# Attention of the latent (MLA) layer: the scaling of the probabilities moved ahead of the row maximum on VectorE, and the next heads' projections spread one to a step

## The reference

```python
def mla_mixer(xn, w_dq, q_norm, w_uq, w_o, k_nope, k_rope, v, cos, sin):
    c_q = rmsnorm(xn @ w_dq, q_norm)
    q = (c_q @ w_uq).reshape(bsz, seq, MLA_HEADS, MLA_NOPE + MLA_ROPE)      # 16 heads, 128 + 64
    q_nope = q[..., :MLA_NOPE]
    q_rope = apply_rope(q[..., MLA_NOPE:], cos[:, None, :], sin[:, None, :])
    # per block of 128 queries
    s = einsum('bqhd,bkhd->bhqk', qn, k_nope) + einsum('bqhr,bkr->bhqk', qr, k_rope)
    s = where(key_pos <= q_pos, s * scale, -inf)
    p = softmax(s, axis=-1)
    o = einsum('bhqk,bkhv->bqhv', p, v)
    return o @ w_o
```

## Time and profile of the kernel before

| | |
|---|---|
| median of 3 runs | 2618.04 us (2617.62 to 2619.24) |
| the profiled execution | 2625.55 us, of which its span 2623.4 us |
| PE busy | 2534.9 us (97% of the span) |
| DVE busy | 1520.8 us (58%) |
| ACT busy | 670.4 us (26%) |
| POOL busy | 1137.1 us (43%) |
| the attention of this layer | from 747 to about 956 us of the span |
| mean granted clock of PE | 0.992 |

### The profile page before, as it was taken

One profiled execution on the slowest core, in us unless ns is written; L12 is line 12 of the kernel. 1 busy time (PEld: TensorE's weight loads), 2 busy tenths in 40 slices (PEclk: granted clock), 3 DMA queues, 4 the chain that ended last, 5 costly groups with the idle time before them and its releaser, 6 DMA issues.

```text
span 2623.4 us, 30947 instructions
## 1 busy us (share of the span) xinstructions
PE 2534.9 (97%) x11668; PEld 2022.2 (77%) x11668; DVE 1520.8 (58%) x2061; ACT 670.4 (26%) x1317; POOL 1137.1 (43%) x765
## 2 busy tenths in 40 slices
PE   8999999999989999999999999999999999999998
PEld 6888888888767778888887777777766667888886
DVE  4764665464675534644746774434446897677721
ACT  2002531021344421200213313333322442222200
POOL 4324455555521225555554453333332224555554
PEclk9999999999999999999999999999999999999999
DMA  6434456655522226655665484454455535665564
GB/s 208 129 97 138 153 189 194 195 192 194 191 92 77 76 86 192 192 192 193 195 207 163 146 249 157 158 161 156 141 181 164 177 110 185 190 195 194 190 195 166
DMA packets 149560, 436.61 MB, mean 166 GB/s; under 512 B 14064, under 2 KB 18352, under 8 KB 149424
## 3 DMA queue, kind: packets, MB, share of 16 engines
q1 hardware_dynamic: 64480, 200.29, 26.0%
q0 software_dynamic: 67840, 201.35, 21.9%
q10 hardware_dynamic: 17104, 33.14, 3.7%
HBM read 417.90 MB, written 16.83 MB: 166 GB/s over the span
## 4 chain that ended last, share of the span: by engine, by line
PE 49%; POOL 18%; issue 18%; DVE 9%; DVEq 2%; ACT 2%; DMA 2%; POOLq 0%; ACTq 0%; SPq 0%
POOL w_lo L424 15%; PE bank L481 12%; PE bank L484 12%; PE bank L483 12%; POOL w_hi L396 4%; PE bank L1142 1%; PE bank L1133 1%; PE bank L958 1%; PE bank L692 1%; DVE rope_sum L2123 1%; DMA projections<-spill_out 1%; PE bank L945 1%; DVE mla_probs L2428 1%; PE bank L1168 1%; DVE ssm_y L2459 1%
## 5 line engine op out<-in xcount | busy, mean ns | idle before, releaser
L424 POOL TENSOR_TENSOR w_lo<-w_raw,w_hi 128x1024 fp32r<-128x1024 f32 x375 | 901.3, 2404 | 11.7 <-DMA w_hi<-stream 3.8
L396 POOL DMA_DIRECT2D w_hi<-stream x376 | 227.2, 604 | 1456.8 <-PE bank L481 1262.3
L481 PE MATMUL bank<-x_hi,w_hi 128*128 128x512 f32 x1464 | 586.4, 401 | 19.2 <-POOL w_lo L410 11.2
L484 PE MATMUL bank<-x_hi,w_lo 128*128 128x512 f32 x1464 | 572.0, 391 | 0.0
L483 PE MATMUL bank<-x_lo,w_hi 128*128 128x512 f32 x1464 | 572.0, 391 | 0.0
L481 PEld LDWEIGHTS bank<-x_hi,w_hi 128*128 128x128 f32 x1464 | 276.0, 189 | 102.3 <-issue 38.8
L484 PEld LDWEIGHTS bank<-x_hi,w_lo 128*128 128x128 f32 x1464 | 275.8, 188 | 59.0
L483 PEld LDWEIGHTS bank<-x_lo,w_hi 128*128 128x128 f32 x1464 | 276.4, 189 | 56.1 <-issue 2.4
L2070 DVE TENSOR_TENSOR relu_sq<-relu 128x512 f32<-128x512 f32 x64 | 181.5, 2837 | 98.0 <-ACT relu L1441 98.0
L481 PE MATMUL bank<-hidden_hi,w_hi 128*128 128x512 f32 x512 | 199.2, 389 | 0.0
L483 PE MATMUL bank<-hidden_lo,w_hi 128*128 128x512 f32 x512 | 199.2, 389 | 0.0
(11 more groups left out here) (440 smaller groups left out, 4488.2 us busy)
## 6 DMA issues: line engine op xcount, KB each, us to landing
w_hi<-stream POOLq DMA_DIRECT2D x376, 512.0 KB, 4.7
w_raw<-stream SPq DMA_DIRECT2D x376, 512.0 KB, 3.7
projections<-spill_out ACTq DMA_DIRECT2D x56, 256.0 KB, 2.1
ssm_x<-projections ACTq DMA_DIRECT2D x4, 1024.0 KB, 7.4
gate_tiles<-projections ACTq DMA_DIRECT2D x16, 256.0 KB, 2.9
ssm_z<-projections ACTq DMA_DIRECT2D x16, 256.0 KB, 2.7
residual<-x_in SPq DMA_DIRECT2D x4, 512.0 KB, 6.6
toeplitz_hi<-toeplitz_rows_hi POOLq DMA_DIRECT2D x4, 512.0 KB, 6.9
```

The costliest lines, as they stand in the source:

```text
L396: e.dma_start(in_slot(whi, t % SLOTS, o), in_stream(o)).then_inc(hi_ready[t % SLOTS], 16)
L424: e.tensor_tensor(wlo[:, s, :], raw[:, s, :], whi[:, s, :].bitcast(F32), ALU.subtract).then_inc(lo_ready, 1)
L481: mm = e.matmul(out, wh, rh, start=first, stop=False)
L484: return e.matmul(out, wl, rh, start=False, stop=last)
```

## The change

It does three things: DVE's scaling of item n - 2 is put ahead of the maximum of item n; the table of units is spread so that no step has two, which puts q1, q2 and q3 in the first three steps of their own block (before it only q3 was there); and rope work is moved one step later on both ACT and DVE. The order in which units follow each other, their number, the banks and the order of the weight tiles stay.

```diff
-        GROUP_STEPS = {3: ["v0"], 4: ["v1", "v2"], 5: ["v3"], 7: ["r0"], 8: ["r1", "k0"], 9: ["k1"], 11: ["k2"],
-                       12: ["k3", "q0"], 13: ["q1"], 15: ["q2"], 0: ["q3"]}
+        GROUP_STEPS = {3: ["v0"], 4: ["v1"], 5: ["v2"], 6: ["v3"], 8: ["r0"], 9: ["r1"], 10: ["k0"], 12: ["k1"],
+                       13: ["k2"], 14: ["k3"], 15: ["q0"], 0: ["q1"], 1: ["q2"], 2: ["q3"]}
...
-                _g = _s // 16 + (0 if _u in ("v0", "v1", "v2", "v3", "q3") else 1)
+                _g = _s // 16 + (0 if _u[0] == "v" or _u in ("q1", "q2", "q3") else 1)
...
-                    if n % 16 in (10, 12) and n < 48:
-                        rope_high(2 * (n // 16 + 1) + n % 16 // 12)
+                    if n % 16 in (11, 13) and n < 48:
+                        rope_high(2 * (n // 16 + 1) + n % 16 // 13)
...
-                    if s in (8, 10):
-                        pair = 2 * g + (s - 8) // 2
+                    if s in (9, 11):
+                        pair = 2 * g + (s - 9) // 2
                         e.wait_ge(rope_raw, pair + 1)
                         exchanged(rraw[pair % 2], 0, 3)
-                    elif s in (9, 11):
-                        rotated(rraw[(s - 9) // 2][:, :]).then_inc(rope_full, 1)
-                    if s in (11, 13):
-                        rope_low(2 * g + (s - 11) // 2)
+                    elif s in (10, 12):
+                        rotated(rraw[(s - 10) // 2][:, :]).then_inc(rope_full, 1)
+                    if s in (12, 14):
+                        rope_low(2 * g + (s - 12) // 2)
...
                 for n in range(MLA_ITEMS + MLA_AHEAD):
-                    if n < MLA_ITEMS:
-                        w = (n % 4 + 1) * P
-                        e.wait_ge(at_s, n + 1)
-                        e.reduce_max(mmx[:, n:n + 1], bank[n % 3][:, 0:w], axis=AX.X)
-                        e.drain()
-                        ts(mnm[:, n:n + 1], mmx[:, n:n + 1], -MLA_SCALE, None, ALU.mult).then_inc(at_m, 1)
                     m = n - 2
                     if 0 <= m < MLA_ITEMS:
                         w = (m % 4 + 1) * P
...
                         e.reciprocal(mri[:, m:m + 1], mrs[:, m:m + 1])
                         e.drain()
                         ts(mpr[:, m % 3, 0:w], mpr[:, m % 3, 0:w], mri[:, m:m + 1], None, ALU.mult).then_inc(at_p, 1)
+                    if n < MLA_ITEMS:
+                        w = (n % 4 + 1) * P
+                        e.wait_ge(at_s, n + 1)
+                        e.reduce_max(mmx[:, n:n + 1], bank[n % 3][:, 0:w], axis=AX.X)
+                        e.drain()
+                        ts(mnm[:, n:n + 1], mmx[:, n:n + 1], -MLA_SCALE, None, ALU.mult).then_inc(at_m, 1)
```

## The result

After: 2621.77 us median (2619.07 to 2629.5, 20 runs); before, timed beside it, 2617.64 (2613.3 to 2621.94, 20 runs). Ratio 1.0017, 95% interval 1.0011 to 1.0023: slower by 2.9 to 6.0 us, forecast +3.8. The single profiled executions say the opposite (span 2618.6 after, 2623.4 before), because in the one of before the granted clock was low for 17 us longer in two stretches that the change does not touch, at 148 and at 1435 us (mean 0.992 against 0.995). So the comparison goes by the timed runs, and the traces are compared over stretches where both had the full clock: from step 7 to step 63 both had it throughout.

What follows compares the result with a forecast made beforehand. PE bounds the attention (busy 50.67 of 54 us), idling mostly for DVE's scaling. Border terms of +5.3 us, less 0.7 and 0.8, gave +3.8 us, carried over to 2621.8; range 2614.5 to 2627.

Steps and rivals of the forecast that it cites:

- The first hold: Scaling of step 8: POOL's subtraction behind r0 holds DVE from 4.54 until 6.92 us after step 7.
- The second hold: Rotation's exchange product, due at 12.0: held by POOL's subtraction behind k0 (11.8 to 14.2), costing 2.1 us.
- DVE's chain: Steps 8 to 13: DVE without pause, 6.92 + 16.2 + 2.1 = 25.2 us; PE would want that scaling at about 20.1.
- The waits: Whole attention: PE's total wait for the scaling about 22 us, not 19.1, plus 2.5 for ACT.
- my walk: Stalls of PE at steps 9, 12, 13 and 14: 1.8, 0.4, 1.8 and 1.0, adding up to 5 us.
- The border: Next block's first scores wait for ACT's copy of q0: 0.9 us at three borders, 2.7 us.
- The order at the quiet places: Two places like step 57, last block: scaling begins 4.54 instead of 4.97 us after scores, gaining 0.4 each, 0.8.
- the first stall: Step 3 of the attention: the maximum of 384 columns goes from in front of the scaling, gaining 0.7 us.
- The sum: Whole program: 2.0 + 2.0 + 1.3 = +5.3, less 0.7 at the start and 0.8 in the last block: +3.8 us.
- holds would miss: Rival: DVE escapes POOL's holds in steps 8 to 13; one missed 2616.1, both 2609.8 us; chance 0.11 each.
- The clock did not fall: Rival was that stalls around step 13 lower the clock: +2 us a block, 2627.8 us; chance 0.09.
- no step with two units: Rival on steps 8 to 13: spreading units makes transposes wait less; equal to holds missing, no separate chance.

Runs made afterwards that it cites:

- the run with small subtractions: After, with POOL subtracting only 8 of 1024 columns in twelve weight tiles and PE reading the high half instead (timing only): 2607.28 us, ratio 0.9959.
- the run that removes it: After, with q0 made in step 14 beside k3 instead of in step 15: 2620.05 us, ratio 1.0001.
- the pair without holds: After and before, each with POOL's subtractions cut to 8 of 1024 columns in twelve tiles: 2607.28 us (ratio 0.9959) and 2609.03 us (0.9961).
- the run with the order alone: Before, with DVE's scaling of item n - 2 put ahead of the maximum of item n and nothing else: 2622.5 us, ratio 1.0014.

## Why the prediction was right

The forecast was 2621.8, within 0.1 us of the measured median, and that is luck: its base was 0.4 us above before's median of the 20 runs, its +3.8 is below the 4.1 between the medians, and the interval is 3 us wide. By its steps:

- **The first hold** was forecast from 4.54 to 6.92 us after step 7 and ran from 4.55 to 6.90 (876.05 and 878.40, less 871.50). Right, and by the mechanism named: the run with small subtractions takes it away (0.42 us).
- **The second hold** was on the rotation's product in step 10, not on a scaling. Right; 2.0 us against 2.1.
- **DVE's chain** to the scaling of step 13: forecast 25.2, measured 24.85 (896.35 less 871.50). The softmax work of five steps was 6.3 us as reckoned; the second hold was 0.1 shorter, the two rotations 0.13 and the two low halves 0.09.
- **The waits**: my walk had 1.8, 0.4, 1.8 and 1.0 and the rows show 1.55, 0.20, 1.60 and 0.75, so PE's total is 18.7, not about 22. As delays the walk was right: against the runs that lack the wait, steps 9, 12, 13 and 14 are longer by 1.75, 0.41, 1.81 and 0.96 us. Each wait delays PE by 0.2 us more than the idle time that the row gives, the border's 0.73 too, and I had taken the one for the other.
- **The border**: forecast 0.9, measured 0.73 idle and 0.94 to 0.96 in all by the run that removes it. Right.
- **The order at the quiet places**: 1.10 became 0.67 at step 57, forecast 0.7; at the first stall 0.7, as forecast, but seen only in the pair without holds, where the clock was full.
- **The sum** over steps 7 to 63: forecast 5.3 less 0.8, +4.5; measured +3.73. With 0.7 for the start, that would be +3.0, against +2.9 to +6.0 timed. These two traces don't show the 0.7: steps 0 to 7 take 14.98 us in before and 15.31 in after, where the granted clock was 0.50 in a second stretch (744 to 747 us). The term that was mis-sized is DVE's chain, by 0.35 us in each of three blocks; the way from its end to step 0 took 0.18 more than reckoned, which with rounding leaves 0.25 a block.
- **The rivals**: that holds would miss did not occur. The clock did not fall in after behind idle of 1.60 us; in the run with the order alone it fell behind 3.06 in one block and not in the next.
- **The reason** needs a correction: I told the loss as one of holds that move, and both kernels pay nearly the same for them (10.3 and 10.9 us). The holds were right in place and length, and still not what makes the change slower.
- **A reading**: I took the exchange of 878.07 as held although it had begun first. Of its three products the first, begun 0.50 us before POOL, ran through in 0.68 us; it is the second, begun 0.20 us after POOL, that was held. DVE from 878.76 on:

```profile
878.76 3.48 DVE L2123 TENSOR_TENSOR rope_sum<-rope_raw,rope_table 32x512 f32<-32x512 f32 x2
```

The Trainium skill ("SBUF — State Buffer", who interferes with whom) has the one that starts first keep the shared ports for its whole instruction, and the other block. The traces agree where POOL's subtraction starts first (876.05, 883.45). Where DVE starts first they show both outcomes. In the run with the order alone the exchange began 0.49 us before POOL's subtraction and its first product was held to that one's end all the same. In before, elsewhere in the program, a DVE operation on two SBUF tiles that began 0.45 us before the subtraction went through, and then the subtraction took 2.48 us where 2.40 is usual:

```profile
1429.29 0.68 DVE L1863 TENSOR_TENSOR x_lo<-next_gained,x_hi 128x512 fp32r<-128x512 f32 x1
...
1429.74 2.48 POOL L424 TENSOR_TENSOR w_lo<-w_raw,w_hi 128x1024 fp32r<-128x1024 f32 x1
...
1429.89 2.88 DVE L2364 SCALAR_TENSOR_TENSOR next_gained<-residual,gain_product,rstd_both 128x512 f32<-128x512 f32 x1
```

So one of the two does block the other, but the recorded starts don't say which, when DVE's lies up to some 0.6 us ahead. What decides there is not shown. POOL's issue of the cast (L396, 0.57 us) stands right ahead of each of these subtractions and had begun before the DVE operation did, in the held cases and in the others, so it doesn't tell them apart either.

The advantage that seemed to lie in the change, no step with two units, is real only where DVE isn't the bound. Between step 8 and the scaling of step 13 DVE has 16 us of work and 4 us of holds, and it can begin only 4.55 us after step 7, while PE by my estimate would want that scaling at 20.1. Spreading PE's units over more steps moved two of them across the border and left PE less to do while it waits.

## What to carry to other kernels

Find the engine without a pause in the stretch where another waits, and sum its work from the last moment at which it was idle: a new order ahead of it moves waits about, and only less work in that stretch removes them. When an instruction is moved that frees a buffer, follow what that release starts on another queue, and look for DVE operations on two SBUF tiles or in-place scalings inside the 2.4 us of such a subtraction on POOL, or begun shortly before it. Count a wait as its idle time and the restart, 0.2 us here. Test the parts of a change one by one and together: here one part won 3.3 us or cost 2.7, with the clock's falls 5.9, depending on the other.

## What the runs showed of the hardware that was not expected

A DVE operation can be held even if it began before POOL's. In the run with the order alone the exchange began at 820.43 and POOL's subtraction at 820.92, and the first product took 3.43 us; in the second block of before, with POOL 0.49 us behind as well (0.491 against 0.485), the first product got through in 0.68. Elsewhere in before a scaling of 512 columns that began 0.64 us ahead (38.62, POOL 39.26) was held too and took 3.35 us. The holds also go the other way: in all kernels, where a DVE product or sum of two SBUF tiles got through that had begun 0.41 to 0.51 us ahead, POOL's subtraction took 2.43 to 2.53 us and ended 2.25 to 2.26 us after it.

A wait of the same 3.06 us on PE was followed in one block by a stretch at a mean granted clock of 0.64 and in the next by one at 1.00. A wait of 2.31 us ahead of step 0 was followed by a clock of 0.50 in after (744 to 747 us) and of 1.00 in before (746.4 to 749.4).
